# Dealing VectorE's modulation chunks unevenly over the blocks of the first projection

## The reference

```python
mod = (silu(c) @ w_ada + b_ada)          # 2048 x 12288, one row
sh1, sc1, g1, sh2, sc2, g2 = split(mod, 6)
h = x * (1 + sc1) + sh1
z = h @ w_in + b_in                      # 2048 -> 9216
z_u, z_v, z_h, z_g = split(z)            # 1024, 1024, 3072, 4096
y_a = spatial_gating(gelu(z_u), gelu(z_v), ...) @ w_branch_a
y_b = hyena(z_h, ...) @ w_branch_b       # short convolution, two long ones by FFT
mix = (sigmoid(z_g)[a] * y_a + sigmoid(z_g)[b] * y_b) @ w_o + b_o
```

## Time and profile before

| | |
|---|---|
| median of three runs | 2608.17 us |
| the profiled execution | 2609.6 us |
| its span, first to last instruction | 2607.8 us |
| mean granted TensorE clock | 0.981 |
| TensorE busy | 2510.8 us, 96% of the span |
| VectorE busy | 2014.3 us, 77% |
| ScalarE busy | 1379.2 us, 53% |
| GpSimd busy | 830.3 us, 32% |
| HBM traffic | 204 GB/s over the span |

### The profile page before, as it was taken

One profiled execution on the slowest core, in us unless ns is written; L12 is line 12 of the kernel. 1 busy time (PEld: TensorE's weight loads), 2 busy tenths in 40 slices (PEclk: granted clock), 3 DMA queues, 4 the chain that ended last, 5 costly groups with the idle time before them and its releaser, 6 DMA issues.

```text
span 2607.8 us, 42659 instructions
## 1 busy us (share of the span) xinstructions
PE 2510.8 (96%) x16524; PEld 2291.1 (88%) x16524; DVE 2014.3 (77%) x2606; ACT 1379.2 (53%) x2169; POOL 830.3 (32%) x765
## 2 busy tenths in 40 slices
PE   6799999999998999999999989999999999999989
PEld 3688888889987888888888879999889999999978
DVE  7889888878889785555555679898868888889855
ACT  0344445444455454445544477776656666666643
POOL 0100011002244520001111239986104666666630
PEclk9799999999999999999999999999999999999989
DMA  9988776787865886556555534445455444444434
GB/s 351 348 298 271 263 251 221 252 278 253 291 227 190 283 280 207 190 178 200 190 192 191 189 122 162 156 159 166 162 164 174 149 152 154 159 157 155 156 111 146
DMA packets 147010, 534.35 MB, mean 205 GB/s; under 512 B 16855, under 2 KB 17016, under 8 KB 146424
## 3 DMA queue, kind: packets, MB, share of 16 engines
q1 hardware_dynamic: 143480, 519.56, 59.6%
q0 software_dynamic: 3328, 12.06, 1.4%
HBM read 525.26 MB, written 6.29 MB: 204 GB/s over the span
## 4 chain that ended last, share of the span: by engine, by line
PE 85%; DVE 7%; issue 3%; DMA 2%; POOL 2%; ACT 1%; SPq 0%; POOLq 0%; DVEq 0%; ACTq 0%
PE ps L610 32%; PE ps L614 26%; PE ps L612 10%; PE ps L613 10%; PE ps L1000 2%; DVE misc L1084 2%; PE ps L672 1%; DMA AF<-in_w_ada 1%; DVE wl L1063 1%; POOL misc L2473 1%; PE ps L701 1%; PE ps L901 1%; PE ps L650 1%; PE ps L732 1%; DMA ring<-in_w_in 1%
## 5 line engine op out<-in xcount | busy, mean ns | idle before, releaser
L1063 DVE TENSOR_TENSOR wl<-ring,wh 128x1024 fp32r<-128x1024 f32 x784 | 1034.5, 1332 | 352.5 <-ACT wh L1819 351.2
L614 PE MATMUL ps<-A,wl 128*128 128x256 f32 x4480 | 1262.2, 282 | 0.0
L1819 ACT CAST wh<-ring 128x1024 fp32r<-128x1024 f32 x784 | 816.0, 1045 | 381.2 <-PE ps L614 361.3
L614 PEld LDWEIGHTS ps<-A,wl 128*128 128x128 f32 x4480 | 855.7, 191 | 0.2
L610 PE MATMUL ps<-A,wh 128*128 128x512 f32 x2176 | 772.2, 399 | 21.3 <-DVE A L1067 7.7
L612 PE MATMUL ps<-A,wh 128*128 128x256 f32 x2304 | 672.8, 292 | 10.3 <-DVE A L1067 9.6
L613 PE MATMUL ps<-A,wh 128*128 128x256 f32 x2304 | 652.6, 283 | 0.0
L610 PE MATMUL ps<-B,wh 128*128 128x512 f32 x1792 | 636.2, 400 | 10.0 <-issue 4.5
L610 PEld LDWEIGHTS ps<-A,wh 128*128 128x128 f32 x2176 | 412.1, 189 | 120.2 <-DVE wl L1063 8.4
L614 PE MATMUL ps<-B,wl 128*128 128x256 f32 x1792 | 501.7, 280 | 0.0
L612 PEld LDWEIGHTS ps<-A,wh 128*128 128x128 f32 x2304 | 442.5, 192 | 12.9 <-issue 10.0
(11 more groups left out here) (253 smaller groups left out, 2245.6 us busy)
## 6 DMA issues: line engine op xcount, KB each, us to landing
ring<-in_w_m SPq DMA_DIRECT2D x256, 512.0 KB, 4.5
ring<-in_hgrn_w_in SPq DMA_DIRECT2D x160, 512.0 KB, 3.8
ring<-in_w_ada SPq DMA_DIRECT2D x146, 512.0 KB, 5.3
ring<-in_w_in SPq DMA_DIRECT2D x144, 512.0 KB, 5.5
ring<-in_conv_w_in SPq DMA_DIRECT2D x96, 512.0 KB, 3.9
AF<-in_w_ada SPq DMA_DIRECT2D x46, 512.0 KB, 8.6
ring<-in_w_ab SPq DMA_DIRECT2D x32, 512.0 KB, 5.9
ring<-in_w_o SPq DMA_DIRECT2D x32, 512.0 KB, 5.7
```

The source lines that it names most:

```text
L614: return e.matmul(dst[:, 0:256], lo, x[:, 0, :], start=False, stop=last)
L1063: e.tensor_tensor(low[:], ring[SLOT[h]][:], hi[:].bitcast(F32), ALU.subtract).then_inc(s.lo, 1)
L1819: e.copy(wh[h % NSPLIT][:], ring[SLOT[h]][:]).then_inc(s.hi, 1)
```

## The change

`chunks_behind` deals the same 72 chunks otherwise. Blocks 3 to 23 keep one each. Of each four blocks of a Hyena pair the first gets two, the second one and the others none; blocks 51 and 55 get one. From block 58 to 71 the even ones get two, the odd ones one, and block 71 two. The sums of groups 5, 6 and 7 move from blocks 33, 49 and 65 to blocks 37, 57 and 67.

```diff
 def chunks_behind(i):
-    return 0 if i < 3 else 2 if 24 <= i < 27 else 1
+    if i < 3:
+        return 0
+    if i < 24:
+        return 1
+    if i < 58:
+        return 1 if i in (51, 55) else (2, 1, 0, 0)[(i - 24) % 4]
+    return 2 if i < 72 and (i % 2 == 0 or i == 71) else 1
...
-    n_ada = {20: 4, 33: 5, 49: 6, 65: 7}
+    n_ada = {20: 4, 37: 5, 57: 6, 67: 7}
```

## The result

| | before | after |
|---|---|---|
| median of six runs | 2608.72 us | 2617.79 us |
| lowest and highest | 2605.45, 2609.82 | 2615.25, 2622.06 |
| the profiled execution | 2609.6 us | 2617.18 us |
| its span | 2607.8 us | 2615.4 us |
| mean granted TensorE clock | 0.981 | 0.981 |

The change makes the kernel slower: the ratio is 1.004 (95% interval 1.003 to 1.005), some 9.1 us. The prediction had 2605.4 us, with a range that ended at 2611.5 us.

A forecast was written before the change was run, and what follows sets the result against it. TensorE is busy 96% of the span, so VectorE changes pay only where TensorE waits for it. 5.9 + 2.1 - 0.7 - 1.1 - 3.4 = 2.8 us less: median 2605.4 us, eight in ten between 2600.0 and 2611.5 us.

The forecast's parts named there:

- First pair: Before block 28's inverse: three chunks fewer ahead of line 1281 end TensorE's wait; gain 4.17 + 1.7 for clock, 5.9 us.
- The rival in which that wait only changes its name: Blocks 27 and 28: late weight halves hold `lo`, 3 to 4 of the 5.9 us stay; about 2609 us, chance 0.10.
- The first rival: All chunks land in time and TensorE's clock stays up at block 52; 6.7 us less, 2601.5 us, chance 0.26.
- Pairs 3 to 6: Later Hyena pairs: line 1281 comes earlier, 3.8 us, less 1.7 for group 6's sum at block 57; gain 2.1 us.
- group 5's sum: Behind block 37's first half: TensorE waits for the second chunk behind block 36; cost 0.7 us, too short to move the clock.
- Sum of group 7, now at block 67: TensorE waits for the second chunk behind block 66: 0.6 us, up to 0.7 more for a late load; cost taken 1.1 us.
- The end of the projection: Behind block 71: the second chunk adds 1.25 us and its load lands late, delaying the low parts; cost taken 3.4 us.
- SyncE's queue: Blocks 58 to 71: chunk loads waiting for slots delay halves about 4.5 and 2 us, covered by existing rest; cost nothing.
- The second rival: Weight halves of blocks 58 to 71 come too late, queue just full at 331 GB/s; 9 us, 2614.5 us, chance 0.12.

The follow-up runs named there:

- x_light: The kernel after, with the 23 chunk loads of blocks 58 to 72 bringing an eighth of their bytes; 2606.44 us, ratio 1.0000 to the kernel before.
- ctl: The kernel after, unchanged, timed again beside the kernel before; 2614.23 us, ratio 1.0033.
- x_order: The kernel after, with odd blocks' chunk loads in blocks 58 to 71 issued behind the two halves instead of ahead; 2612.52 us, ratio 1.0024.
- x_early: The kernel after, with the 22 chunks of blocks 58 to 71 dealt two each behind 58 to 65, one each behind 66 to 71; 2608.22 us, ratio 1.0005.

## Why the prediction was wrong

**First pair: right.** -5.9 us predicted, -6.2 measured in all runs. Block 28's inverse did not wait, and the clock held there. The rival in which that wait only changes its name is out. The first rival is out too: the chunks did not land in time, and even x_light, where nearly all did, is level with the kernel before and not 6.7 us under it, since blocks 32 to 58 gave it nothing.

**Pairs 3 to 6 and group 5's sum: right in kind, the gain not seen.** Three inverse waits were left, 4.8 us in all, the longest 1.6 us; before, these pairs had four, 6.7 us in all. The five waits for `wl` in blocks 44 to 52, 3.1 us, took more than that back, and the term has no such wait. The sum of group 5 waited 0.83 us where 0.7 were predicted. Net, the stretch 32 to 58 gave nothing where 1.4 us were forecast; but the eight kernels that deal this stretch alike (the one after and all named x or ctl) show -1.8 to +2.3 us there, with a median of +0.1, so the forecast lies inside what one execution can show.

**"Sum of group 7, now at block 67": the first failed term.** It was put at 1.1 us and its stretch cost 8.3: 4.0 us of wait, 3.4 of clock, and 0.7 of a wait for line 1323. The premise that failed is "There VectorE is on time". It had waited 4.44 and 1.75 us for chunks behind blocks 62 and 64, and it evicted block 66 1.8 us later behind TensorE's end of that block than it did block 70 before. The load of the sum's last chunk went out only when VectorE had added the chunk behind block 65, at 555.2 us, and was wanted 4.3 us later instead of 5.4. It took 5.8 us, still within the 3.8 to 6.1 us of the earlier trace rows. So the 4.0 us are about 0.6 of VectorE's own work, which the term had, 1.8 of lateness brought along and 1.5 of landing, for which it had up to 0.7. Where the earlier trace rows did mislead is further up: they belong to a queue at a share of 0.85, and from 525 to 537 us, at 1.00, the chunk of block 62 took 8.7 us. x_light, with lighter loads, shrank the wait from 4.0 to 0.8 us. The step also gave the wait no price in clock.

**"The end of the projection": the second failed term.** 3.4 us predicted, 6.0 measured in the wait and 6.5 in the stretch. Its pieces are 1.25 us for the chunk and 2.92 us for its landing, which the term had right in kind (1.25, and 1.1 to 2.7), and 1.3 us with which VectorE arrived late out of block 70, plus 0.5 us of line 1368, which it left out. The load itself took 6.7 us, as in the earlier trace rows. The 1.3 us have two parts, the wait of 1.22 us for block 70's second chunk and, ahead of it, 0.7 us by which VectorE evicted block 70 later than usual, behind a half for which ScalarE had waited 2.0 us; some of it was caught up. x_light's handover is 2.6 us longer than before. That lies within what the term gives, but by other pieces: its last load was waited for only 0.5 us.

**"SyncE's queue. … I cost it at nothing": the step beneath both.** The cover named for it, rest on VectorE ahead of each eviction and halves cast 3 us after they land, was true of the kernel before. It is gone: ScalarE waited 17.5 us for halves. The step also looked only at who waits for the halves. No wait of TensorE in blocks 58 to 71 of the kernel after is one for a half. What the step left out is the queue that all loads share: 22 chunks instead of 14 go in these blocks beside the same 28 halves, the share rose to 0.93 and 1.00 over 513 to 537 us, and chunks landed late. x_order had nearly all halves in time and still lost at the sum; x_light had the chunks light and did not lose.

**The second rival had the right place and the wrong carrier.** It said that weight halves come too late at 331 GB/s and put that at 2614.5 us, chance 0.12; measured 2617.79. It stands nearer to the measured time than the forecast does, but its mechanism is not the one that ran, and its slack of 1.3 us per two blocks has no row. The rate was right: 320 to 338 GB/s at shares of 0.93 to 1.00. In the kernel after not the halves but the chunks made TensorE wait, save for the part of 0.7 us above. In x_early, with a denser load, both did. It was given a small chance because of the 405 GB/s of the kernel's first stretch. The windows of 12 us shown here at a share of 0.99 to 1.00 have 338 and 350 GB/s, and one further on in x_early 368. The row that should have been used stood in the same group: 281 GB/s at 0.85 makes 331 at 1.00. The rate at full share is no constant, though; four microseconds in the kernel after reach 418. x_early, then the kernel after:

```profile
564.00:576.00 12.00, 12.00 (x71) 10.61 (x70) 9.89 (x11) 7.37 (x10) 0.00 (x0) 1.00 1.00 368
```

```profile
585.50:589.50 4.00, 4.00 (x24) 3.44 (x23) 2.17 (x4) 2.45 (x4) 0.00 (x0) 1.00 1.02 418
```

The page "DMA: Bandwidth & Descriptors" of the Trainium skill, section "Where 436 GB/s comes from", gives about 358 GB/s as the bound for transfers between HBM and the core's own memory. As a mean over 12 us of a full queue that is within 6% of these three windows, a better guide than the row from the start. As a bound the runs do not bear it out: 368, 405 and 418 GB/s lie above it.

## What to carry to other kernels

Work that is dealt out in a stretch with time to spare is only free if its loads are: before moving chunks, compute the share of the DMA engines that the new place will have, and do not take landing times from a stretch with a lower one. An operation that waits for a load holds up everything behind it on its engine, so look for the next thing TensorE wants from that engine, above all a sum or a handover right behind a doubled block. A deadline one block later was worth some 7 us here, and the variant that owed one chunk less and repaid at once, in the next blocks that have time, kept all of the gain.

## What the runs showed of the hardware

The granted clock does not follow the length of a wait alone. Waits of 0.83 us stand ahead of the sum of group 5 at block 37 in two kernels. After:

```profile
350.58 1.95 PE L658 MATMUL ps<-ones,XR 128*128 128x1 f32 x16 [0.83 <-DVE XR L1092]
```

```profile
354.00:358.00 4.00, 4.00 (x24) 3.47 (x23) 1.93 (x4) 2.31 (x5) 0.00 (x0) 1.00 1.00 337
```

x_light:

```profile
349.45 2.58 PE L659 MATMUL ps<-ones,XR 128*128 128x1 f32 x16 [0.83 <-DVE XR L1093]
```

```profile
353.00:357.00 4.00, 4.00 (x12) 3.27 (x11) 0.94 (x3) 1.31 (x2) 0.00 (x0) 0.50 0.97 347
```

The same wait and the same instructions, and behind them the clock stays at its upper level (2.4 GHz) in one and stands at its lower (1.2 GHz, 0.50) for four microseconds in the other. In x_early a wait of 2.55 us left it at 1.00:

```profile
542.00:546.00 4.00, 3.64 (x22) 3.25 (x23) 3.44 (x6) 2.69 (x5) 0.00 (x0) 1.00 0.64 230
```

The prediction had read from the earlier trace rows that a wait under 1.3 us is too short to move the clock. A short wait can cost 2 to 3 us more in one execution and nothing in another, which may be part of why the runs of one kernel spread over 4 to 10 us here; that was not measured by itself.
